# Two pairs of attentions, each run as one row of alternating units

## What is computed

```
# first network, layer 0, 8 heads: a latent query sees 256 latent keys (with a bias) and 256 context keys
s = concat([q @ k_band * scale + bias, q @ k_ctx * scale]);  latent = softmax(s) @ [v_band, v_ctx]
# the same layer: a context query sees the 256 context keys
context = softmax(q_ctx @ k_ctx * scale) @ v_ctx
# second network, layer 0: differential attention, 4 heads, values of 128 columns, causal
diff = (softmax(q1 @ k1 * scale) - lam * softmax(q2 @ k2 * scale)) @ v      # then an RMS norm over each head
# the same layer: causal attention, 8 heads
causal = softmax(q @ k * scale) @ v
```

## Time and profile before

| | us |
|---|---|
| median of 3 runs | 2728.82 (2723.95 to 2730.58) |
| the profiled execution | 2726.7 |
| its span, first to last instruction | 2724.9 |
| latent attention, first scores to last values | 213.9 to 264.4 |
| context attention | 264.4 to 309.0 |
| differential attention with its norm | 1884.2 to 1914.9 |
| causal attention | 1914.9 to 1955.1 |

### The profile page before, as it was taken

The page is one execution under the profiler, slowest core; times in us unless marked ns, Lnnn a source line. Parts: engine busy times, 40 slices in busy tenths (PEclk is TensorE's granted clock), DMA queues, the critical chain, the costliest instruction groups (busy, mean ns, idle before and its releaser), DMA issues.

```text
span 2724.9 us, 47547 instructions
## 1 busy us (share of the span) xinstructions
PE 2438.2 (89%) x20564; PEld 1986.5 (73%) x20564; DVE 1729.1 (63%) x3304; ACT 998.6 (37%) x1864; POOL 65.0 (2%) x70
## 2 busy tenths in 40 slices
PE   7699978999988996888889788988979999997998
PEld 6365447877865596778788588987668879667886
DVE  6876259676646246667774578765455876654577
ACT  1004333323322113435432155343334654553465
POOL 0300000000000000000000000011000001000000
PEclk9798799999998998999999999988679999997999
DMA  7450025655542100000001257842034863102475
GB/s 291 154 185 32 16 77 202 245 216 203 214 162 78 47 1 1 3 3 3 3 11 64 80 215 266 299 165 92 0 124 170 327 227 120 54 1 89 173 296 200
DMA packets 47281, 348.05 MB, mean 128 GB/s; under 512 B 5248, under 2 KB 5248, under 8 KB 5728
## 3 DMA queue, kind: packets, MB, share of 16 engines
q1 hardware_dynamic: 45936, 334.52, 33.0%
q0 software_dynamic: 1136, 10.50, 1.0%
HBM read 343.95 MB, written 1.05 MB: 127 GB/s over the span
## 4 chain that ended last, share of the span: by engine, by line
PE 72%; DVE 21%; ACT 4%; issue 2%; DMA 1%; DVEq 0%; ACTq 0%; POOLq 0%
PE banks L533 20%; PE banks L926 8%; PE banks L1784 4%; DVE arena L611 4%; PE banks L1660 3%; PE banks L1021 3%; PE banks L2529 3%; PE banks L2530 3%; PE banks L2531 3%; PE banks L1000 3%; PE banks L786 2%; PE banks L1855 2%; PE banks L1254 2%; PE banks L2560 1%; PE banks L1010 1%
## 5 line engine op out<-in xcount | busy, mean ns | idle before, releaser
L611 DVE SCALAR_TENSOR_TENSOR arena<-weight_slots,silu_c,arena 128x256 f32<-128x256 f32 x776 | 329.0, 496 | 0.0
L514 DVE TENSOR_TENSOR moe_w_low<-weight_slots,moe_w_high 128x2048 fp32r<-128x2048 f32 x96 | 218.0, 2289 | 73.0 <-ACT moe_w_high L505 72.1
L926 PE MATMUL banks<-arena,weight_slots 128*128 128x256 f32 (+1 forms) x768 | 231.8, 460 | 19.0 <-DVE arena L1578 11.7
L926 PEld LDWEIGHTS banks<-arena,weight_slots 128*128 128x128 f32 x768 | 149.8, 196 | 97.0 <-issue 75.3
L514 DVE TENSOR_TENSOR mlp_w_low<-weight_slots,mlp_w_high 128x2048 fp32r<-128x2048 f32 x64 | 146.3, 2286 | 106.8 <-ACT mlp_w_high L505 106.7
L505 ACT ACTIVATE moe_w_high<-weight_slots 128x2048 fp32r<-128x2048 f32 x96 | 181.2, 1910 | 26.2 <-PE banks L2562 19.8
L1784 PE MATMUL banks<-weight_slots,arena 64*64 64x64 f32 (+1 forms) x3648 | 151.0, 225 | 36.8 <-DVE weight_slots L2097 15.5
L505 ACT ACTIVATE mlp_w_high<-weight_slots 128x2048 fp32r<-128x2048 f32 x64 | 122.2, 1910 | 159.1 <-PE banks L533 140.9
L1784 PEld LDWEIGHTS banks<-weight_slots,arena 64*64 64x64 f32 x3648 | 141.8, 136 | 44.9 <-issue 16.3
L2529 PE MATMUL banks<-moe_w_high,slots_x 128*128 128x512 f32 x320 | 133.6, 417 | 11.8 <-DVE moe_w_low L514 11.8
L1936 ACT ACTIVATE weight_slots<-banks 128x512 f32<-128x512 f32 x80 | 47.8, 598 | 231.6 <-DVE weight_slots L2097 203.3
(11 more groups left out here) (371 smaller groups left out, 5275.2 us busy)
## 6 DMA issues: line engine op xcount, KB each, us to landing
weight_slots<-weights SPq DMA_DIRECT2D x318, 1024.0 KB, 4.9
arena<-small POOLq DMA_DIRECT2D x1, 2560.0 KB, 9.1
arena<-x_t POOLq DMA_DIRECT2D x1, 2048.0 KB, 16.4
arena<-bias POOLq DMA_DIRECT2D x1, 2048.0 KB, 9.4
constants<-consts POOLq DMA_DIRECT2D x1, 1395.0 KB, 21.1
out_t<-arena SPq DMA_DIRECT2D x1, 1024.0 KB, 3.9
parameters<-params POOLq DMA_DIRECT2D x1, 775.0 KB, 9.7
arena<-pool_inv POOLq DMA_DIRECT2D x1, 512.0 KB, 10.3
```

The lines of the kernel that those rows point to most:

```text
L514: nc.vector.tensor_tensor(self.pair(j)[1], slot(j, 0, SLOT), self.pair(j)[0], ALU.subtract).then_inc(*v.step("used", j))
L611: nc.vector.scalar_tensor_tensor(a_, w, c, a_, ALU.mult, ALU.add).then_inc(*v.step())
L926: ins = nc.tensor.matmul(psum(b, 0, w), slot(j, k, 256, i * P, P), moving(k), start=(k == 0), stop=(k == KT - 1))
```

## The change

The four calls become two. A new class `Interleaved` holds a list of (attention, unit) pairs, its row, and passes every question (scores, masks, blocks, values, where the result goes) to the attention that owns the unit; `factor` and `subtract`, which were attributes, become methods, since they now differ from unit to unit. `LAT_CON` takes latent and context units by turns (32 units, latent first). `DIF_CAU` takes differential and causal units by turns for 16 units, then the last 8 causal units (24 in all). The norm of the differential heads moves to turns inside that row, on PE, ACT and DVE, by a `between` argument. What each unit computes, and with which instructions, is the same.

```diff
-        def att_tensor(pe, A):
+        def att_tensor(pe, A, between={}):
...
                 if 0 <= i - 3 < A.n:
                     values(i - 3)
+                if i in between:
+                    between[i]()
+                    pe.stage(A.name)
...
+        class Interleaved(Attention):
+            def __init__(self, name, base, place_free, row):
+                self.name, self.base, self.place_free, self.row, self.n = name, base, place_free, row, len(row)
+            def scores(self, u):
+                a, own = self.row[u]
+                return a.scores(own)
...
+        LAT_CON = Interleaved("latent_context_attention", ATT_A, ("bias",), [(a, u) for u in range(16) for a in (LAT, CON)])
...
+        DIF_CAU = Interleaved("causal_attentions", ATT_B, ("e2_roped", 15),
+                              [(a, u) for u in range(8) for a in (DIF, CAU)] + [(CAU, u) for u in range(8, 16)])
...
-        def subln_scalar(act):
+        def subln_squares_scalar(act):
             act.stage("head_norm")
-            act.wait_ge(*act.own)
+            act.wait_ge(*after("taken", DIF_CAU.name, "out", 14))
             for h in range(4):
                 nc.scalar.activation(RAW[:, h], OB[:, h], ACT.Square).then_inc(*act.step("head_square", h))
+        def subln_roots_scalar(act):
+            act.stage("head_norm")
             load_table(act, ACT.Sqrt)
...
+            load_table(act, ACT.Exp)
...
-            att_tensor(pe, LAT)
-            att_tensor(pe, CON)
+            att_tensor(pe, LAT_CON)
...
-            att_tensor(pe, DIF)
-            subln_tensor(pe)
-            att_tensor(pe, CAU)
+            att_tensor(pe, DIF_CAU, {19: lambda: subln_tensor(pe)})
...
-            att_scalar(act, DIF)
-            subln_scalar(act)
-            att_scalar(act, CAU)
+            att_scalar(act, DIF_CAU, {17: lambda: subln_squares_scalar(act), 20: lambda: subln_roots_scalar(act)})
...
-            att_vector(v, DIF)
-            att_vector(v, CAU, {3: lambda: subln_vector(v, 0), 6: lambda: subln_vector(v, 1),
-                                9: lambda: subln_vector(v, 2), 12: lambda: subln_vector(v, 3)})
+            att_vector(v, DIF_CAU, {21: lambda: subln_vector(v, 0), 22: lambda: subln_vector(v, 1),
+                                    23: lambda: subln_vector(v, 2), 24: lambda: subln_vector(v, 3)})
```

More of the change, by code:

```diff
@@ L1070, in weights @@
                 v.wait_ge(*v.own)
-                if A.factor is not None:
-                    f = A.factor(u)
+                f = A.factor(u)
+                if f is not None:
                     nc.vector.tensor_tensor(M[:, u % 3, 9:9 + k], M[:, u % 3, 9:9 + k], f, ALU.mult).then_inc(*v.step())
                     v.wait_ge(*v.own)
-                if A.subtract:
+                if A.subtract(u):
                     (c0, w), (c1, _) = maps
@@ L1093, in att_vector, with att_scalar @@
                     between[i]()
-        def att_scalar(act, A):
+        def att_scalar(act, A, between={}):
             act.stage(A.name)
@@ L1137, in att_scalar @@
                     out(i - 3)
+                if i in between:
+                    between[i]()
+                    act.stage(A.name)
             act.mark(A.name, "done")
         class Attention:
-            factor = None
             filled = False
-            subtract = False
             pre, post = 1.0, HD ** -0.5
@@ L1154, in values_ready, with factor, subtract, ready @@
                 return ()
+            def factor(self, u):
+                return None
+            def subtract(self, u):
+                return False
+        class Interleaved(Attention):
+            def __init__(self, name, base, place_free, row):
+                self.name, self.base, self.place_free, self.row, self.n = name, base, place_free, row, len(row)
+                self.pre, self.post = row[0][0].pre, row[0][0].post
+                assert all((a.pre, a.post) == (self.pre, self.post) for a, _ in row)
+            def ready(self, u):
+                a, own = self.row[u]
+                return a.ready(own)
+            def values_ready(self, u):
+                a, own = self.row[u]
+                return a.values_ready(own)
+            def factor(self, u):
+                a, own = self.row[u]
+                return a.factor(own)
+            def subtract(self, u):
+                a, own = self.row[u]
+                return a.subtract(own)
+            def scores(self, u):
+                a, own = self.row[u]
+                return a.scores(own)
+            def pieces(self, u):
+                a, own = self.row[u]
+                return a.pieces(own)
+            def maps(self, u):
+                a, own = self.row[u]
+                return a.maps(own)
+            def blocks(self, u):
+                a, own = self.row[u]
+                return a.blocks(own)
+            def values(self, u):
+                a, own = self.row[u]
+                return a.values(own)
+            def place(self, u):
+                a, own = self.row[u]
+                return a.place(own)
         def half(h):
@@ L1366, in place @@
                 return CAT[half(h), CTX, 4 + h // 2, qt * P:(qt + 1) * P]
-            place_free = ("latent_attention", "done")
         LAT, CON = LatentAttention(), ContextAttention()
+        LAT_CON = Interleaved("latent_context_attention", ATT_A, ("bias",), [(a, u) for u in range(16) for a in (LAT, CON)])
         H8 = area(25088, KT, 2 * SEQ)
@@ L2320, in bass_two_blocks @@
             name, n, base = "causal_attention", 16, ATT_B
-            place_free = ("differential_attention", "done")
             def ready(self, u):
@@ L2352, in bass_two_blocks, with subtract @@
             name, n = "differential_attention", 8
-            subtract = True
-            place_free = ("e2_roped", 15)
+            def subtract(self, u):
+                return True
             def factor(self, u):
@@ L3100, in _ @@
             ev_in_tensor(pe)
-            att_tensor(pe, LAT)
-            att_tensor(pe, CON)
+            att_tensor(pe, LAT_CON)
             pool_tensor(pe)
-            cat_ready = lambda k: [("pool_done",), ("context_attention", "done")]
+            cat_ready = lambda k: [("pool_done",), (LAT_CON.name, "done")]
             project_tensor(pe, "x01", "ev_out", lambda k: CAT[:, :, k, :], cat_ready, BOTH,
@@ L3119, in _ @@
             lambda_tensor(pe)
-            att_tensor(pe, DIF)
-            subln_tensor(pe)
-            att_tensor(pe, CAU)
+            att_tensor(pe, DIF_CAU, {19: lambda: subln_tensor(pe)})
             project_tensor(pe, "x21", "ev2_out", lambda k: CAT2[:, k, :],
-                           lambda k: [("causal_attention", "done"), ("head_normed", 3)], ONE, banks=range(6),
+                           lambda k: [(DIF_CAU.name, "done"), ("head_normed", 3)], ONE, banks=range(6),
                            then=x_sums(pe, "n2_2"))
@@ L3143, in _ @@
             ev_out_of(act, 0, act_copy)
-            att_scalar(act, LAT)
-            att_scalar(act, CON)
+            att_scalar(act, LAT_CON)
             pool_scalar(act)
@@ L3220, in _ @@
             mod_vectors(v, 0, range(2, 6))
-            att_vector(v, LAT)
-            att_vector(v, CON)
+            att_vector(v, LAT_CON)
             v.stage("norm")
```

## The result

| | before | after |
|---|---|---|
| median | 2727.57 us of 4 runs (2723.95 to 2730.58) | 2752.63 us of 4 (2751.2 to 2773.75) |
| the profiled execution, its span | 2726.7, 2724.9 | 2752.76, 2751.0 |
| first pair, first scores to pooling | 213.95 to 309.02, 95.1 | 215.65 to 337.10, 121.4 |
| second pair, first scores to projection | 1884.16 to 1955.10, 70.9 | 1910.00 to 1981.90, 71.9 |
| mean granted clock | 0.934 | 0.924 |

Ratio to the kernel before 1.0107, with its 95% interval in brackets [1.0082, 1.0131]: slower by 1.1% (the medians alone stand 0.9% apart). The forecast was 2753.

What follows compares the result with a forecast made beforehand. The prediction took PE, at half clock, to bound the first row and the second row's mixed part. +27.5 us and -2.3 us made +25.2: 2751.9 from the profiled 2726.7, 2754.0 from the median; forecast 2753, range 2722 to 2757.

Steps and rivals of the forecast that it cites:

- Half clock for nearly the whole row: First row, latent and context units alternating: PE's clock falls at the start and stays at 0.50 for at least 13 pairs.
- The piece between scores goes with the return: First row: PE's 2.10 and 2.52 us between scores lie between 1.67 (clock stayed half) and 2.95 (returned); half clock taken.
- +27.5 us for the first pair: Latent and context attention as one alternating row at half clock: 122.6 us against 95.1 before.
- The 0.9 us that the sum took off: First row's start: 0.9 us subtracted because PE works twice as fast between the first weights and the clock's fall.
- 2753 for the whole: Whole kernel: +25.2 us on the profiled 2726.7 gives 2751.9, from the median 2754.0; 2753 taken.
- Each pair at the full clock is 5.44, not 4.2: First row at full clock: the loop over DVE, ACT and PE sets 5.44 us a pair, not PE's 4.2.
- rival 1: First row: clock returns within the first five pairs; both pairs together -6.9 us, about 2722, or 2719 without a fall; chance 0.15.
- Rival 3: First row: clock returns early and the loop does not bind, 4.2 us a pair; total 2705; chance 0.04.
- -2.3 us for the second pair: Differential and causal attention as one row: 68.6 us against 70.9, handover removed, head norms in the tail.
- PE's sums of 3.8 us cover them but for about 1 us: Second row's tail: PE's head sums hide most of ACT's two table loads and four roots, about 4.5 us.
- Rival 4: Second row's tail costs more than the handover did: +2.5 instead of -2.3 us, total 2758; chance 0.03 above 2758.
- The rule named in the prediction: Clock gate: sustained matmul activity releases the throttle, so busy PE soon runs at full speed; first row would give 90.5 us.

## Why the prediction was right, and where it was not

- **Half clock for nearly the whole row.** Right, and the whole of the result: 116.05 of 121.4 us.
- **The piece between scores goes with the return.** The prediction had 1.67 us without a return and 2.95 with one, and chose a side for what lies between. The runs agree: with pieces of 2.95 us the clock came back after 10.2 us twice more, with 2.10 and 2.52 not once while scores were left, in four rows (the change and three variants, 116 to 123 us each), and in the row with filling matmuls after 13.65. Whether the length of the piece is what counts, or something that goes with it, no run separates. It explains only the return. The step that said the context attention stays at half because of its pieces is half of the truth: it also had to enter the stretch at half, and where it entered at full (in four experiments) it stayed at full. The likeness of the share of scores in all three rows, 40%, was rightly put aside: the shift by one turn leaves that share as it is.
- **+27.5 us for the first pair.** Measured +26.4. The start (4.5 us to the first transposes, against 4.4) and the pair (7.75 against 7.77) were as summed. The 0.9 us that the sum took off, for work at the full clock behind the first weights, was not there: the clock fell at 218.41, while PE still waited for them. Against that stand the last 2.64 us at the full clock, which the sum had at half.
- **2753 for the whole.** Measured 2752.63, and that close by luck: on the profiled execution the first row was summed 1.1 us too high, the second 3.3 too low, and 1.2 us, which nothing forecast, were given back elsewhere in the span. That the first row sets the result, and its size within 1.1 us, is not luck.
- **Each pair at the full clock is 5.44, not 4.2.** Right, with 5.29; so rival 1's row, 87.8 to 90.5 us, is what the filled start gave (88.1).
- **Rival 3's 4.2 us a pair** needs the loop away, and the shift by one turn came to 4.36. Its reason against, the queue of ACT, was right for the change as made.
- **-2.3 us for the second pair.** Wrong: +1.0. The step that failed is "PE's sums of 3.8 us cover them but for about 1 us". The table loads stand on ACT behind the exponential of unit 20, which needs that unit's scores, which stand behind the sums on PE. So ACT is idle during the sums and begins when they are over; the roots then hold the four banks. Price 2.84 us. Before the change nothing stood between the squares and that load, so it ran beside the sums (1911.99, in 1911.10 to 1914.88); the sum carried this overlap over to a queue that no longer has it. With the roots one turn earlier the row came to 68.4, against the 68.6 of the sum: the gain of the removed handover is real, and small. That the two agree so well is partly luck, since a pair in the mixed part took 4.9 to 5.0 us (four score groups from 1931.52 to 1941.40, the next four to 1951.48), not 4.8, PE's waits for DVE came to 4.8 us, not 3, and 6.83 us behind the sums ran at the full clock, which the sum had at half. Rival 4 had this tail's direction, at +2.5.
- The rule named in the prediction, of the Trainium skill's page "TensorE: Matmul & The Clock Gate", section "The HAM clock gate", again did not carry over: 114.19 us busy of 116.05 did not release the clock, and 8.39 of 10.23 did.

## What to carry to other kernels

Before reordering PE's work, read the granted clock over each stretch, and what PE did just before it fell; where a row is at half clock with PE busy, look first for the short stretch of light work in front of it, and fill that, even with matmuls whose result nobody reads (18 us here for eight of them, without a new order; in the alternating row the clock still fell, but for 3.42 us only). When two streams are merged at a fixed lag, check which kinds of work the lag brings together: the same alternation took 121 or 76 us for a lag of 3 or 4. And when work is said to be hidden under another engine's, follow its own queue back to see that nothing ahead of it waits for that same work.

## What the runs showed of the hardware

**The clock fell with PE shown busy without a gap.** In the run with the sums in two banks it fell at 216.1. Its PE timeline, and windows up to and over the fall:

```profile
204.77 9.23 PE L1326 MATMUL banks<-weight_slots,arena 128*128 128x256 f32 x42
213.83 3.00 PE L630 MATMUL banks<-constants,arena 128*128 128x1 f32 x24
216.77 4.63 PE L1000 MATMUL banks<-arena 64*128 64x512 f32 x6
```

```profile
214.00:216.10 2.10, 2.10 (x22) 2.10 (x21) 0.69 (x1) 0.00 (x0) 0.00 (x0) 1.00 0.41 90
216.10:216.77 0.67, 0.67 (x6) 0.66 (x5) 0.00 (x0) 0.00 (x0) 0.00 (x0) 0.53 0.98 416
```

Ahead of the first scores PE does 24 matmuls of one column each, 3.00 us that the profile shows as busy; the fall came inside them. The Trainium skill, same page, section "HAM oscillation", lays a renewed throttle on idle time such as a wait for a DMA; this fall had none in front of it. In the other kernels where it fell at this start, it came during or after the three score groups, where these, the scores and the wait for the first weights follow each other; in three of the four with a filled start it did not fall. How much each of the three adds was not tried, nor whether the DMA traffic of that moment (a share of 0.98 from 216.10 on) has a part.

A second fall of this kind is in the profiled run of the shift by one turn, far from the change. PE is shown busy without a gap from 2274 on, and the clock falls at 2287.72, at the end of 32 matmuls of 48 columns:

```profile
2284.18 3.67 PE L2936 MATMUL banks<-parameters,arena 128*128 128x48 f32 x32
```

```profile
2284.18:2287.72 3.54, 3.54 (x34) 3.54 (x32) 2.06 (x6) 0.37 (x1) 0.00 (x0) 1.00 0.00 0
2287.72:2287.85 0.13, 0.13 (x3) 0.13 (x3) 0.00 (x0) 0.00 (x0) 0.00 (x0) 0.51 0.00 0
```

In the run with the second pair apart the same 32 matmuls, again 3.67 us, were followed by work at the full clock. So such matmuls stood in front of both falls, but they do not always bring one.

**The time of one kernel can have two values by where the clock falls elsewhere.** The profiled run of the shift by one turn took 2725.09 us and a second one 2729.22, four others 2703.7 to 2706.0. Its chain in the matmuls that follow this second fall, which compress the keys and values of a later attention:

```profile
2287.85 27.33 PE banks L3031 x128
```

In the run with the second pair apart the same 128 matmuls took 14.30 us, at 1.00. In the slow one the clock stayed at 0.50 from the fall on for 47.78 us, with PE busy all the time. The 2773.75 of the changed kernel, a 2770.86 with the roots beside the sums, and 2752.61 and 2757.31 with a fill in every turn stand 19 to 24 us above their fellows in the same manner. No profile was taken of those, so that it is the same place is only likely.
